# Attention by pairs of heads on the two halves of the TensorE array

## What is computed

```python
def gqa_attend(q, k, v):
    s = jnp.einsum('bqhgd,bkhd->bhgqk', q, k).astype(F32) * (q.shape[-1] ** -0.5)
    p = jax.nn.softmax(s, axis=-1).astype(v.dtype)
    o = jnp.einsum('bhgqk,bkhd->bqhgd', p, v)
...
        s_loc = jnp.einsum('bqhd,bqkhd->bhqk', qi, kg).astype(F32) * scale + rpb_flat[:, bi].astype(F32)[None]
        s_ctx = jnp.einsum('bqhd,bchd->bhqc', qi, kc).astype(F32) * scale
        p = jax.nn.softmax(jnp.concatenate([s_loc, s_ctx], axis=-1), axis=-1).astype(v.dtype)
```

## Time and profile before

| | |
|---|---|
| three runs, us | 4103.49, 4108.5, 4110.19 |
| median, us | 4108.5 |
| span of the profiled execution, us | 4099.3 |
| TensorE busy | 3802.5 us, 93% of the span |
| VectorE, ScalarE, GpSimd busy | 35%, 27%, 26% |
| the four stretches of attention | 558.3 us together |

### The profile page before, as it was taken

The page is one execution under the profiler, slowest core; times in us unless marked ns, Lnnn a source line. Parts: engine busy times, 40 slices in busy tenths (PEclk is TensorE's granted clock), DMA queues, the critical chain, the costliest instruction groups (busy, mean ns, idle before and its releaser), DMA issues.

```text
span 4099.3 us, 47988 instructions
## 1 busy us (share of the span) xinstructions
PE 3802.5 (93%) x20075; PEld 2883.8 (70%) x20075; DVE 1453.9 (35%) x2019; ACT 1102.5 (27%) x1722; POOL 1065.4 (26%) x635
## 2 busy tenths in 40 slices
PE   6979999989999999979999978899899999998998
PEld 2855555767766777768888866777677667666886
DVE  3762222312456311232222267533314463123222
ACT  2421111112354311122222143221122543123322
POOL 3221111232102111232222331332233021234443
PEclk8989999999999999989999988899999999998999
DMA  5122323011001122212222221000021012332331
GB/s 181 47 65 89 103 88 98 1 48 51 21 5 28 59 56 61 72 36 62 67 61 64 62 67 46 1 1 1 2 76 42 1 32 82 93 98 72 94 98 62
DMA packets 304645, 234.92 MB, mean 57 GB/s; under 512 B 16628, under 2 KB 274898, under 8 KB 303792
## 3 DMA queue, kind: packets, MB, share of 16 engines
q1 hardware_dynamic: 298992, 207.68, 17.4%
q0 software_dynamic: 5440, 24.18, 2.1%
HBM read 223.31 MB, written 12.44 MB: 58 GB/s over the span
## 4 chain that ended last, share of the span: by engine, by line
PE 87%; DVE 5%; issue 3%; DMA 2%; ACT 2%; POOL 1%; SPq 0%; ACTq 0%; POOLq 0%; DVEq 0%
PE ps L362 15%; PE ps L364 15%; PE ps L363 15%; PE ps L656 5%; PE ps L433 5%; PE ps L419 3%; PE ps L550 3%; PE ps L439 3%; PE ps L561 3%; DMA wring<-in_w_mod 2%; PE ps L552 2%; PE ps L373 2%; PE ps L591 2%; PE ps L592 2%; PE ps L608 1%
## 5 line engine op out<-in xcount | busy, mean ns | idle before, releaser
L362 PE MATMUL ps<-hh,wh 128*128 128x512 f32 (+1 forms) x2592 | 948.8, 366 | 105.8 <-DVE hl L995 79.0
L1341 POOL TENSOR_TENSOR wl<-wring,wh 128x1024 fp32r<-128x1024 f32 x264 | 643.5, 2441 | 1376.3 <-ACT wh L794 1376.1
L363 PE MATMUL ps<-hl,wh 128*128 128x512 f32 (+1 forms) x2592 | 918.0, 354 | 0.0
L364 PE MATMUL ps<-hh,wl 128*128 128x512 f32 (+1 forms) x2592 | 917.0, 354 | 0.0
L362 PEld LDWEIGHTS ps<-hh,wh 128*128 128x128 f32 x2592 | 499.2, 193 | 201.5 <-issue 63.0
L363 PEld LDWEIGHTS ps<-hl,wh 128*128 128x128 f32 x2592 | 499.9, 193 | 73.7 <-issue 9.6
L364 PEld LDWEIGHTS ps<-hh,wl 128*128 128x128 f32 x2592 | 498.8, 192 | 67.6
L794 ACT ACTIVATE wh<-wring 128x1024 fp32r<-128x1024 f32 x264 | 277.5, 1053 | 911.8 <-DMA wring<-in_w_in 463.3
L362 PE MATMUL ps<-fh,wh 128*128 128x512 f32 (+1 forms) x768 | 275.0, 358 | 0.0
L364 PE MATMUL ps<-fh,wl 128*128 128x512 f32 (+1 forms) x768 | 274.7, 358 | 0.0
L1276 DVE SCALAR_TENSOR_TENSOR R<-ps,modcs,R 128x512 f32<-128x512 f32 x216 | 136.3, 659 | 388.9 <-PE ps L364 388.7
(11 more groups left out here) (214 smaller groups left out, 5158.2 us busy)
## 6 DMA issues: line engine op xcount, KB each, us to landing
wring<-in_w_ffn SPq DMA_DIRECT2D x128, 512.0 KB, 4.0
wring<-in_w_in SPq DMA_DIRECT2D x116, 512.0 KB, 3.8
wring<-in_w_mod SPq DMA_DIRECT2D x96, 512.0 KB, 4.5
wring<-in_w_branch SPq DMA_DIRECT2D x48, 256.0 KB, 4.3
wring<-in_w_out SPq DMA_DIRECT2D x16, 512.0 KB, 4.1
R<-bias_skewed POOLq DMA_DIRECT2D x32, 224.0 KB, 4.0
x_store<-R POOLq DMA_DIRECT2D x2, 3072.0 KB, 10.2
R<-x_store POOLq DMA_DIRECT2D x2, 3072.0 KB, 10.7
```

The costliest lines, as they stand in the source:

```text
L362: mm(ps[:, t0:t1], ahk, rh[:, k, t0:t1], start=(k == 0), stop=False)
L363: mm(ps[:, t0:t1], ahk, rl[:, k, t0:t1], start=False, stop=False)
L364: last = mm(ps[:, t0:t1], alk, rh[:, k, t0:t1], start=False, stop=(k == kn - 1))
L1341: G.tensor_tensor(slot_view(wl, n % NSPL, l, name, i), w, slot_view(wh, n % NSPL, l, name, i).bitcast(F32), ALU.subtract)\
```

## The change

The list of items now goes by pairs: for heads 2p and 2p + 1 and each block t, the item of the even head and that of the odd one stand side by side. TensorE's loop takes a pair a turn. It takes the PSUM tiles of both before the first product. The scores are issued a, b, a, b (512 keys of each, then 256 of each), on the lower and the upper half of the array's rows. The values are issued a, b in turn for each of the 6 (or 2) blocks; head b's output now goes to partitions 64 to 127, so that the two use the two halves of the array's columns, and ScalarE reads it from there. The transposes of a and then of b follow. The list of operations on ScalarE and VectorE and its order within an item stay as they are, except that the items come in the new order. The bias tables get four buffers, and from head 4 on a table waits for the last item that read its buffer.

```diff
         def att_items(l):
-            return [(h, t) for h in range(A_H) for t in range(TT if l == 0 else LT)]
+            return [(2 * hp + u, t) for hp in range(A_H // 2) for t in range(TT if l == 0 else LT) for u in range(2)]
...
-                for i in range(len(work) + 4):
+                for i in range(0, len(work) + 4, 2):
                     if i < len(work):
-                        h, t = work[i]
+                        t = work[i][1]
...
-                        ps = take(pe, "S", br, l, i)
-                        if t < LT:
-                            mm(ps[:, 0:LAT], qs, k[lo:lo + HD, kc, 0:LAT], start=True, stop=True)
-                            last = mm(ps[:, LAT:TOK], qs, k[lo:lo + HD, kc, LAT:TOK], start=True, stop=True)
-                        else:
-                            last = mm(ps[:, 0:CTX], qs, k[lo:lo + HD, kc, LAT:TOK], start=True, stop=True)
-                        last.then_inc(*filled("S", br, l, i))
+                        ps = [take(pe, "S", br, l, i + u) for u in range(2)]
+                        for c0, n0, n1 in ((0, 0, LAT), (LAT, LAT, TOK)) if t < LT else ((0, LAT, TOK),):
+                            for u in range(2):
+                                h, lo = work[i + u][0], HD * u
+                                kc = 4 + h // 4 if br == "A" else h // 2
+                                last = mm(ps[u][:, c0:c0 + n1 - n0], q[lo:lo + HD, h // 2, t * P:t * P + P],
+                                          k[lo:lo + HD, kc, n0:n1], start=True, stop=True)
+                                if n1 == TOK:
+                                    last.then_inc(*filled("S", br, l, i + u))
                     if i >= 2:
-
-                        ps = take(pe, "T", br, l, i - 2)
+                        ps = [take(pe, "T", br, l, i - 2 + u) for u in range(2)]
+                        last = [None, None]
                         if i >= 4:
...
-                            pe.wait_ge(*read("T", br, l, i - 4))
+                            b0 = 0 if work[i - 4][1] < LT else LT
+                            for u in range(2):
+                                pe.wait_ge(*read("T", br, l, i - 4 + u))
                             for b in range(b0, TT):
...
+                                for u in range(2):
+                                    h, lo = work[i - 4 + u][0], HD * u
+                                    c0 = HD * (h // 4 if br == "A" else h)
+                                    last[u] = mm(ps[u][lo:lo + HD, TOK:TOK + P], v[:, b, c0:c0 + HD],
+                                                 probT[:, (i - 4 + u) % 3, b - b0, :], start=(b == b0), stop=(b == TT - 1))
+                        for u in range(2):
+                            if i - 2 < len(work):
+                                nk = TT if work[i - 2][1] < LT else TT - LT
+                                pe.wait_ge(*dve_done.at("prob", br, l, i - 2 + u))
+                                for b in range(nk):
+                                    last[u] = tr(ps[u][:, b * P:b * P + P], prob[:, u, b * P:b * P + P], ident)
+                            last[u].then_inc(*filled("T", br, l, i - 2 + u))
...
-                                             pair("T", br, l, j)[0:HD, TOK:TOK + P], ACT.Copy)\
+                                             pair("T", br, l, j)[lo:lo + HD, TOK:TOK + P], ACT.Copy)\
...
-                    if h >= 2:
-                        pool.wait_ge(*read("S", "B", l, per * (h - 1) - 1))
+                    if h >= 4:
+                        pool.wait_ge(*read("S", "B", l, 2 * per * (h // 2 - 1) - 2 + h % 2))
...
-                        pool.dma_start(ebias[u * 64:u * 64 + 64, h % 2, :, :], src).then_inc(*e_in.mark(l, h, by=16))
+                        pool.dma_start(ebias[u * 64:u * 64 + 64, h % 4, :, :], src).then_inc(*e_in.mark(l, h, by=16))
```

More of the change, by code:

```diff
@@ L176, in program @@
         probT = r(S0 + 16128, 3, TT, P)
-        ebias = r(S0, 2, 14, GRID_W)
+        ebias = r(S0, 4, 14, GRID_W)
         stat = sb("stat", [P, 2, 4])
@@ L424, in attention @@
                     if i >= 2:
-                        ps = take(pe, "T", br, l, i - 2)
+                        ps = [take(pe, "T", br, l, i - 2 + u) for u in range(2)]
+                        last = [None, None]
                         if i >= 4:
-                            h, t = work[i - 4]
-                            b0 = 0 if t < LT else LT
-                            c0 = HD * (h // 4 if br == "A" else h)
-                            pe.wait_ge(*read("T", br, l, i - 4))
+                            b0 = 0 if work[i - 4][1] < LT else LT
+                            for u in range(2):
+                                pe.wait_ge(*read("T", br, l, i - 4 + u))
@@ L432, in attention @@
                             for b in range(b0, TT):
-                                last = mm(ps[0:HD, TOK:TOK + P], v[:, b, c0:c0 + HD], probT[:, (i - 4) % 3, b - b0, :],
-                                          start=(b == b0), stop=(b == TT - 1))
-                        if i - 2 < len(work):
-                            nk = TT if work[i - 2][1] < LT else TT - LT
-                            pe.wait_ge(*dve_done.at("prob", br, l, i - 2))
-                            for b in range(nk):
-                                last = tr(ps[:, b * P:b * P + P], prob[:, i % 2, b * P:b * P + P], ident)
@@ L440, in attention @@
-                        last.then_inc(*filled("T", br, l, i - 2))
+                                for u in range(2):
[10 more added lines that the diff above has]
+                            last[u].then_inc(*filled("T", br, l, i - 2 + u))
@@ L1012, in attention @@
                             V.tensor_tensor(ps[:, 0:LAT], ps[:, 0:LAT],
-                                            ebias[:, h % 2, 6 - 2 * t + 0:14 - 2 * t, :].rearrange("p a b -> p (a b)"),
+                                            ebias[:, h % 4, 6 - 2 * t + 0:14 - 2 * t, :].rearrange("p a b -> p (a b)"),
                                             ALU.add).then_inc(*dve_done.mark("bias", l, i))
@@ L1469, in bias @@
                         src = toeplitz[15 * h + 1 - u:15 * h + 15 - u].rearrange("j c k -> c j k")
-                        pool.dma_start(ebias[u * 64:u * 64 + 64, h % 2, :, :], src).then_inc(*e_in.mark(l, h, by=16))
+                        pool.dma_start(ebias[u * 64:u * 64 + 64, h % 4, :, :], src).then_inc(*e_in.mark(l, h, by=16))
                     pool.wait_ge(*e_in.at(l, h))
-                    e = ebias[:, h % 2, :, :]
+                    e = ebias[:, h % 4, :, :]
                     G.tensor_tensor(e, e, cst[:, C_MASK:C_MASK + GRID_W].unsqueeze(1).to_broadcast([P, 14, GRID_W]), ALU.add)\
                         .then_inc(*pool_done.mark("E", l, h))
-                for h in range(2):
-                    bias(h)
-                for h in range(2, B_H):
+                for h in range(B_H):
                     bias(h)
```

3 lines of the change are left out of this document (removed).

## The result

| | before | changed |
|---|---|---|
| median, us | 4107.43 (4 runs, 4103.49 to 4110.19) | 4144.22 (4 runs, 4127.06 to 4152.65) |
| ratio, 95% interval | | 1.0086 [1.0063, 1.0109] |
| the same kernels again, us | 4103.92 | 4133.63 (6 runs, 4124.81 to 4144.99) |
| ratio | | 1.0073 [1.0060, 1.0087] |
| span of the profiled execution | 4099.3 | 4125.2 (4137.7 in the second measurement) |

The change makes the kernel slower by 37 us (30 in the second measurement). The prediction had the sign, and the range 4120 to 4400 holds the time. But its forecast, 4196, was a loss of 88 us. The profiled execution of the changed kernel was the fastest of its four, 26 us longer in span than that of the kernel before.

A forecast was written before the change was run, and what follows sets the result against it. PE was taken to bound the attentions; pairing would add ScalarE waits. Span 4099.3 + 14 at full clock + 74 for the clock = 4187, and 4196 as median of runs; range 4120 to 4400 us.

The forecast's parts named there:

- Today PE sets the pace; nothing outside the attentions moves.: Four attentions: PE busy 547.5 of 558.3 us, so it sets the pace; nothing outside them is touched.
- ScalarE's chain behind transposes a: Latent pairs: exponential a, two copies, exponential b take 3.15 us, leaving PE idle 2.2 to 2.5 us per pair.
- Products of the pair, 1.91 and 1.57: Latent pair on PE: with overlap, scores take 1.91 us and values 1.57, giving a period of 7.43 against 7.48.
- rival 4: Pair products: heads wholly independent, period under 7.3 us; 4079 us, or 4150 if the clock falls; chance 0.04.
- Rivals 1: Pair products: neither scores nor values overlap, +145 us and clock +83, giving 4350 us; chance 0.20.
- rival 2: Pair products: only one kind overlaps, 4285 us for scores alone or 4258 for values alone; chance 0.17.
- rival 5: Pair products: every alternation between heads pays the change of form, above 4400 us; chance 0.03.
- VectorE is not late.: Attentions: VectorE is busy 322 of 558 us, its work lying beside PE's values and transposes a.
- The bias tables, +6: Start of B: the first pair needs tables 0 and 1, VectorE waits some 3 us a layer, +6 us.
- Sum at full clock, +14: Attentions at full clock: latent pairs -3, context queries +11, bias tables +6, together +14 us.
- The clock, 64 idles at 1.15, +74: Latent pairs: each of 64 idles brings 3.4 us at half clock, losing 1.15 us each, +74 us.
- Attention of layer 0 grows more than that of layer 1.: Attentions by layer: layer 0, which alone has context queries, should grow more than layer 1; no size given.

The follow-up runs named there:

- Experiment 7: New item list and four bias buffers, but TensorE takes one item a turn as in the kernel before; 4120.66 us, 1.0039 of the kernel before.
- Experiment 2: Changed kernel with ScalarE doing both exponentials before the copies of a and b, still two probability buffers; 4122.94 us, 1.0044 of the kernel before.
- experiment 3: Changed kernel with four probability buffers instead of two, ScalarE's order unchanged; 4088.07 us, 0.9961 of the kernel before.
- experiment 1: Changed kernel with head a's latent scores computed twice more in TensorE's idle time, then overwritten; 4138.45 us, 1.0083 of the kernel before.
- experiment 6: Changed kernel issuing both score products of head a, then both of head b; 4148.63 us, 1.0097 of the kernel before.
- experiment 4: Changed kernel with four probability buffers, ScalarE's exponentials before copies, VectorE's bias, maximum and scaling of both heads first; 4029.08 us, 0.9814 of the kernel before.
- experiment 8: Bias table 0 made before A, in three kernels: changed 1.0070, one item a turn in the new order 1.0047, all three edits 0.9815 of the kernel before.
- experiment 9: The changed kernel run again without any edit, for its spread and the clock's price; 1.0073 of the kernel before, six runs spread over 20.2 us.
- experiment 5: Changed kernel with both heads' values sent to partitions 0 to 63, the same half of the columns; 4237.4 us, 1.0324 of the kernel before.

## Why the prediction was right and wrong, step by step

- **Today PE sets the pace; nothing outside the attentions moves.** Held as far as the profile can tell.
- **The new order of items by itself, no term.** This was missing. Experiment 7 has the order without the pairing and is 16 us slower than the kernel before, about half of the whole loss if the two add up, which no run shows.
- **ScalarE's chain behind transposes a, 3.02 to 3.30 us, and PE idle for 2.2 to 2.5 in each pair.** Right: 3.1, and 2.33 us before each pair of scores of A. Experiments 2 and 3 each loosen one part of the chain and the idle of A goes to 1.48 and 1.37; experiment 1 fills it and the period stays. In B the buffer is not the limit (experiment 3: 7.17 as before the edit).
- **Products of the pair, 1.91 and 1.57.** Wrong in size: 1.49 and 1.46. The failing sentence is "Issued in order, each head's second instruction must wait for its first; the other head's first goes beside it". The two heads don't hold each other up at all, and experiment 6 shows that even four instructions of a ahead of b don't. With the chain at 3.1 for 3.15, the period of a latent pair was 6.81 in A, not 7.43. The products alone are what rival 4 had, with a period of 6.76 in all.
- **Rivals 1, 2 and 5 (no overlap, one kind only, alternation drains).** All wrong. The Trainium skill's statement that a change of tile alone drains nothing (TensorEngine Tiling (Array Packing), Key Properties) agrees with the trace: 24 alternating value products take the 1.46 us that 12 took.
- **"VectorE is not late."** Right in A, not in B. There it adds the bias as well, transposes b wait 0.40 us for its scaling in half of the pairs, and the period is 7.17; with four probability buffers it is 7.17 still (experiment 3), and 6.47 once VectorE takes both heads' bias and maximum first (experiment 4, with the other two edits). Timeline, B of layer 1:

```profile
3408.69 1.53 PE L434 MATMUL ps<-R 128*64 128x128 f32 x24
...
3411.43 0.77 PE L441 MATMUL ps<-cst,R 128*128 128x128 f32 x5 [0.40 <-DVE R L1031]
```

- **The bias tables, +6.** Too dear. VectorE waits 2.32 us for table 1 in layer 0 and not at all in layer 1. With table 0 early (experiment 8) the second transposes of B come 1.8 us sooner after the first scores in layer 0 and 0.4 in layer 1; the 1.8 may be too low by up to 1.5, since that start stood at half clock (5.41 us for the same 16 score instructions, against 3.88).
- **Sum at full clock, +14.** By the price of experiment 9, 0.36 to 0.43: the attentions spent some 89 us more at half clock than before (128 against 39, from clocks of 0.97, 0.97, 0.96 and 0.96), worth 32 to 38 us; they grew by 19. At full clock they would have been some 13 to 19 us shorter than before. In the second execution it is 118 us more, worth 42 to 51, grown by 31.5, so 11 to 19 shorter; this is no second proof, as the 0.43 comes from these two executions. Of this, 32 pairs of A at 6.81 and 32 of B at 7.17 instead of 7.48 make -31; context pairs, fills, drains and starts of B are the other +12 to +20, where the prediction had +17.
- **The clock, 64 idles at 1.15, +74.** Right in kind, since by these estimates the clock is what makes the kernel slower, but too dear: 32 to 51. The price of a fall was near: 1.15 us for 3.4 at half clock, 0.34 for each (3.4 x 0.69 / 2 is 1.17, in fact), where 0.36 to 0.43 was measured. The number of falls was not: 64 of them are 218 us at half clock, and 89 to 118 came on top. The step that failed is the one from "they are over 1.96" to the same fall behind each of the 64. In the middle of A in layer 1 the idle of 2.33 comes before every pair and the clock never falls (window; the clock is the 1.00):

```profile
3223.00:3298.00 75.00, 49.30 (x484) 36.93 (x484) 39.66 (x88) 41.91 (x89) 0.00 (x0) 1.00 0.00 1
```

  It falls behind starts and drains and at context turns, and in B where a second wait stands near the first; 10.2 us at half clock follow the start of B, and 6.8 follow a scaling that took 2.27 us beside GpSimd's addition of a table. Windows, B of layer 1:

```profile
3320.84:3331.08 10.24, 7.24 (x41) 4.86 (x39) 6.53 (x14) 3.38 (x6) 5.19 (x4) 0.50 0.20 46
3348.14:3354.96 6.82, 5.38 (x24) 3.40 (x26) 3.26 (x7) 2.07 (x4) 3.22 (x3) 0.50 0.29 70
```

  And the timeline there:

```profile
3345.85 2.27 DVE L1031 TENSOR_SCALAR R<-R,stat 128x768 f32<-128x768 f32 x1
...
3348.17 1.11 PE L441 MATMUL ps<-cst,R 128*128 128x128 f32 x4 [2.04 <-DVE R L1031]
```

  The clocks forecast for the attentions, 0.75 to 0.9, came out at 0.84 to 0.94 (0.81 to 0.93 in the second execution). The Trainium skill's advice on idle gaps (TensorE: Matmul & The Clock Gate, Why this matters for your kernels) agrees with these idles of 2.33, and it does not agree with the 1.19 us of experiment 8, behind which 16.9 us at half clock stand, nor with experiment 5, where the clock fell in eight of eleven turns with the same 2.33.
- **Attention of layer 0 grows more than that of layer 1.** Right: +20 against -1 us.

So two terms were too dear: at full clock -11 to -19 came where +14 was expected, with the other sign, and the clock cost 32 to 51 where 74 was expected. A third, the cost of the new order without the pairing, was not there at all; it lies within these figures. Rival 4, heads wholly independent, ended with "if the clock falls as well it is 4150 and belongs to the forecast". That is the case that came, at 4134 to 4144. Its number is near in part by luck: it stands for -29 at full clock and +74 for the clock, and both are larger than what came. The prediction should have asked which of its two answers on overlap (in order, or independent) carried the forecast; it gave nearly all of the chance to the first, on no row.

What stays open: which idles take the clock down. A rule by the length of an idle alone is excluded: 2.33 didn't in the middle of A, the same 2.33 did in experiment 5, and 1.19 did in experiment 8. More work between the idles is no cure either: in experiment 5 TensorE had 1.3 us more of it in each turn. How much of the 12 to 20 us of fills, drains and context turns belongs to each wasn't settled.

## What to carry to other kernels

When two streams of work are paired on one engine, follow every buffer that the pair shares: with two buffers for a pair, the double buffering of the single items is gone, and the next engine's chain (here exponential, two copies, exponential) stands in the open. Give the pair four buffers and issue all first steps before all second steps on the engines behind; here that turned +0.8% into -1.9%. Four buffers alone gave -0.4%, by A; what each of the two orders adds on top was not measured apart. And price a clock that falls from executions of the same program, and count its falls apart from its price: one for each idle was about twice too many. Then try the new order of work without the pairing: here it cost 16 us by itself.

## What the runs showed of the hardware

- Float32 products on two halves of the rows (64x512) or of the columns (128x128) overlap entirely: 1.49 us for two heads where one takes 1.48, and 1.46 where one takes 1.46. When the values share the same columns, they take 2.76 us and the kernel is 100 us longer.
- They overlap without being issued alternately (experiment 6: 1.50 us). In the kernels of experiments 7 and 8 with one item a turn, the first two score items of B already lie side by side (x4 in 1.14 us).
- The fill of A in layer 0 was followed by 10.1 us at half clock in the kernel before and 20.4 in that of experiment 8, with TensorE busy throughout both; the idle before it was 1.97 us in the one and 3.26 in the other. In layer 1 it was 1.96 and 3.26, with 0.96 for the whole of A in both kernels.
- Idles of 2.33 us before the scores of each pair: no fall of the clock in eleven turns of the changed kernel, a fall of 3.4 us in eight of eleven turns of experiment 5, each 1.6 us longer for it (9.75 for 8.11).
- A VectorE scaling of 128x256 took 2.12 us beside a GpSimd addition of 2.07, against 0.47 alone.
